# Two transformer blocks on one core: the modulation's products moved from VectorE to f32 matmuls in four column groups

## The reference

```python
c_act = jax.nn.silu(c)                       # [1, 2048]
mod = c_act @ w_ada[l] + b_ada[l]            # w_ada: [2048, 12288], 100.7 MB
sh1, sc1, gt1, sh2, sc2, gt2 = jnp.split(mod, N_MOD, axis=-1)
h = modulate(rmsnorm(x, g_norm_mix[l]), sh1, sc1)     # h * (1 + scale) + shift
proj = h @ w_in[l]
...                                          # conv, gated recurrence, pooling
x = x + gt1[:, None, :] * y                  # y = mixed @ w_out
h = modulate(rmsnorm(x, g_norm_ffn[l]), sh2, sc2)
f = (jax.nn.silu(h @ w_ffn_gate[l]) * (h @ w_ffn_up[l])) @ w_ffn_down[l]
x = x + gt2[:, None, :] * f
```

## Time and profile before

| | |
|---|---|
| median of three runs | 2662.82 us |
| span of the profiled execution | 2662.5 us |
| its time beyond the span | none is reported apart; the span is 0.3 us under the median |
| PE busy | 2521.5 us, 95% |
| DVE busy | 1904.7 us, 72% |
| ACT busy | 1183.1 us, 44% |
| moved by DMA | 553.91 MB, mean 208 GB/s |

### The profile page before, as it was taken

How to read it: one execution, slowest core, us unless ns; L and a number is a source line. 1 busy time by engine, 2 the same in 40 slices (tenths; PEclk the granted TensorE clock), 3 DMA queues, 4 the chain that set the end, 5 groups by cost and what they waited for, 6 DMA issues and landing times.

```text
span 2662.5 us, 38962 instructions
## 1 busy us (share of the span) xinstructions
PE 2521.5 (95%) x14020; PEld 2142.7 (80%) x14020; DVE 1904.7 (72%) x2383; ACT 1183.1 (44%) x1437; POOL 9.8 (0%) x37
## 2 busy tenths in 40 slices
PE   1399998999999999999999999999999999999997
PEld 0286676888888888888888888888888888888886
DVE  7899887865555555577677565576788758875886
ACT  1154434444444444464344455455544444444443
POOL 1000000000000000000000000000000000000000
PEclk9999998999999999999999999999999999999998
DMA  9888996965555555565555455565555555565553
GB/s 359 328 314 286 341 335 231 338 214 185 186 187 183 189 184 188 162 193 180 172 177 168 160 169 191 190 183 190 180 186 185 189 180 185 182 196 182 189 170 114
DMA packets 158485, 553.91 MB, mean 208 GB/s; under 512 B 18337, under 2 KB 22433, under 8 KB 158385
## 3 DMA queue, kind: packets, MB, share of 16 engines
q1 hardware_dynamic: 156384, 549.85, 60.8%
q0 software_dynamic: 848, 2.69, 0.3%
q10 hardware_dynamic: 1152, 0.03, 0.0%
HBM read 550.38 MB, written 2.10 MB: 208 GB/s over the span
## 4 chain that ended last, share of the span: by engine, by line
PE 89%; DVE 8%; issue 2%; ACT 1%; DMA 1%; DVEq 0%; SPq 0%; ACTq 0%
PE ps L499 54%; PE ps L501 27%; DVE acc L1104 4%; PE ps L494 2%; PE ps L496 1%; PE pm L534 1%; DVE split L1060 1%; PE pm L544 1%; DMA x_t<-in_x_fm 0%; ACT split L764 0%; DVE xc L1259 0%; DVE ssq L1141 0%; PE pm L649 0%; DVE val L1175 0%; PE pm L594 0%
## 5 line engine op out<-in xcount | busy, mean ns | idle before, releaser
L1060 DVE TENSOR_TENSOR split<-raw,split 128x1024 fp32r<-128x1024 f32 (+1 forms) x864 | 1032.3, 1203 | 660.4 <-ACT split L764 658.2
L764 ACT ACTIVATE split<-raw 128x1024 fp32r<-128x1024 f32 (+1 forms) x864 | 897.7, 1043 | 1205.0 <-PE ps L501 1106.0
L499 PE MATMUL ps<-h_s,split 128*128 128x512 f32 x3904 | 1383.6, 399 | 16.1 <-DVE h_s L1169 7.2
L501 PE MATMUL ps<-h_s,split 128*128 128x256 f32 x3904 | 1094.4, 280 | 0.0
L499 PEld LDWEIGHTS ps<-h_s,split 128*128 128x128 f32 x3904 | 734.8, 188 | 208.9 <-issue 20.0
L499 PE MATMUL ps<-mid_s,split 128*128 128x512 f32 x2368 | 836.9, 399 | 0.2 <-DVE split L1060 0.2
L501 PEld LDWEIGHTS ps<-h_s,split 128*128 128x128 f32 x3904 | 738.6, 189 | 0.5
L501 PE MATMUL ps<-mid_s,split 128*128 128x256 f32 x2368 | 663.5, 280 | 0.0
L499 PEld LDWEIGHTS ps<-mid_s,split 128*128 128x128 f32 x2368 | 444.8, 188 | 121.8 <-issue 12.1
L501 PEld LDWEIGHTS ps<-mid_s,split 128*128 128x128 f32 x2368 | 446.8, 189 | 0.0
L771 ACT ACTIVATE low<-ps 128x512 f32<-128x512 f32 x224 | 129.9, 580 | 4.4 <-PE ps L501 4.4
(11 more groups left out here) (222 smaller groups left out, 1155.2 us busy)
## 6 DMA issues: line engine op xcount, KB each, us to landing
raw<-in_w_in SPq DMA_DIRECT2D x224, 512.0 KB, 3.3
ride<-in_w_ada_late SPq DMA_DIRECT2D x128, 512.0 KB, 5.6
raw<-in_w_ffn_down SPq DMA_DIRECT2D x128, 512.0 KB, 3.3
raw<-in_w_ffn_gate SPq DMA_DIRECT2D x88, 512.0 KB, 3.3
raw<-in_w_ffn_up SPq DMA_DIRECT2D x88, 512.0 KB, 3.4
raw<-in_w_ffn_a SPq DMA_DIRECT2D x88, 512.0 KB, 4.1
raw<-in_w_ffn_b SPq DMA_DIRECT2D x88, 512.0 KB, 4.4
ada<-in_w_ada SPq DMA_DIRECT2D x64, 512.0 KB, 5.8
```

Of the source, the lines that this page charges most:

```text
L499: pe.matmul(ps[:, s, b, :], split[:, slot, k, 0, b * P:(b + 1) * P], acts[:, k0 + k, :, :].rearrange("p h t -> p (h t)"), start=start, sto ...
L501: mm = pe.matmul(ps[:, s, b, 0:T], split[:, slot, k, 1, b * P:(b + 1) * P], acts[:, k0 + k, 0, :], start=False, stop=stop)
L764: act.activation(split[:, c, 0:kt, 0, :], raw[:, CHUNKS * s + c, 0:kt, :], ACT.Copy).then_inc(hi_ready, 1)
L1060: dve.tensor_tensor(split[:, c, 0:kt, 1, :], raw[:, CHUNKS * s + c, 0:kt, :], split[:, c, 0:kt, 0, :].bitcast(F32), ALU.subtract).then_inc ...
```

## The change

- All 12 parts are multiplied on PE. A piece is now two row tiles, 1 MB, and there are 96 of them (8 for each part). For each of its two row tiles `e` and column halves `h`, one f32 product with a stationary operand of 32 columns (`c_pad`: column 0 is the activation's, 31 are zero) writes 32 partitions of one PSUM bank, from partition 32 * (2h + e). So the four products of a piece lie in four column groups of the array.
- At a part's end ACT copies the bank to `row` (128 by 512), and four f32 products with the two-column selector `sel` add the two row tiles and turn the row; DVE adds the bias. The row's DMA is gone.
- Before slab 0 come the parts in the order 2, 0, 3, 1, with a ring of 5 pieces. Parts 2 and 0 are scale and shift of features 0 to 1023, so the first 8 blocks are normed before the other two parts are in.
- The 64 later pieces ride at 8 in 12 chunks (parts 4 to 9 in `ADA_ORDER`'s order, from slab 0) and then 8 in 16 chunks (slabs 20 to 28), with a ring of 3.
- The last part alone keeps the old layout in memory; its pieces are read with a stride of 8 elements.
- The first norm's sum of squares and the pooling's products change PSUM banks.

```diff
-def _rides():
-    at = {S: ([0, 1, 2, 3], []) for S in range(5)}
-    at.update({5: ([0, 1, 2, 3], [3]), 6: ([0, 1, 2, 3], [1, 2, 3])})
...
+    for n in range(EARLY, ADA_PARTS):
+        if n < 10:
+            at += [12 * (n - EARLY) + d for d in (0, 1, 2, 4, 5, 6, 8, 9)]
+        else:
+            at += [CHUNKS * 20 + 20 * (n - 10) + 2 * d for d in range(PIECES)]
...
+        for piece in range(EARLY * PIECES):
+            if piece >= EARLY_RING:
+                sp.wait_ge(ada_multiplied, piece - EARLY_RING + 1)
+            load_ada(piece % EARLY_RING, piece // PIECES, piece % PIECES)
...
+            for r, at in enumerate(RIDE_AT):
+                if at == G - RAW:
+                    sp.wait_ge(ada_multiplied, EARLY * PIECES + max(r - LATE_RING + 1, 0))
+                    load_ada(r % LATE_RING, EARLY + r // PIECES, r % PIECES)
...
+        def multiply_ada(n, i, slot, times):
+            if i == 0 and n > 0:
+                pe.wait_ge(row_copied, n)
+            pe.wait_ge(ada_loaded[slot], 16 * times)
+            piece = ada_slot(slot)
+            for e in range(2):
+                for h in range(2):
+                    g = 32 * (2 * h + e)
...
+                    mm = pe.matmul(pm[2][g:g + 32, :], c_pad[:, 2 * i + e, :], moving,
+                                   start=(i == 0), stop=(i == PIECES - 1))
+            mm.then_inc(ada_multiplied, 1)
+        def turn_ada(n):
+            pe.wait_ge(row_copied, n + 1)
+            if n >= 1:
+                pe.wait_ge(mod_ready, n)
+            for j in range(4):
+                mm = pe.matmul(pm[3][:, 2 * j:2 * j + 2], row[:, j * P:(j + 1) * P], sel[:, :], start=True, stop=True)
+            mm.then_inc(ada_turned, 1)
...
+        def ride_along(G):
+            for r, at in enumerate(RIDE_AT):
+                if at == G:
...
+                    multiply_ada(EARLY + r // PIECES, r % PIECES, slot, before + r // LATE_RING + 1)
+            for n, at in LAST_RIDE.items():
+                if at + 2 == G:
+                    turn_ada(n)
...
+        def copy_row(n):
+            act.wait_ge(ada_multiplied, PIECES * (n + 1))
+            if n >= 1:
+                act.wait_ge(ada_turned, n)
+            act.activation(row[:, :], pm[2][:, :], ACT.Copy).then_inc(row_copied, 1)
...
-        for k in range(DB):
-            add_first(0, k)
...
+        finish_ada(0)
+        finish_ada(1)
+        dve.wait_ge(mod_ready, 2)
+        modulated_gain(1, "g_norm_mix", 0, LB)
+        norm(0, 0, range(LB))
+        finish_ada(2)
```

More of the change, by code:

```diff
@@ L64 @@
 ADA_PARTS = N_MOD * D // ADA_COLS
-ADA_FIRST = 4
-ADA_RING = 8
-RIDE_RING = 5
-def _rides():
-    at = {S: ([0, 1, 2, 3], []) for S in range(5)}
-    at.update({5: ([0, 1, 2, 3], [3]), 6: ([0, 1, 2, 3], [1, 2, 3])})
[L74 to L79, removed]
-RIDE_AT = _rides()
[L83 to L109, removed]
+ADA_FIRST = ADA_PARTS - 1
+RIDE_PARTS = range(ADA_FIRST, ADA_PARTS)
+ADA_ORDER = (2, 0, 3, 1, 4, 5, 8, 6, 9, 7, 10, 11)
+PIECES = DB // 2
+EARLY = 4
+EARLY_RING = 5
+LATE_RING = 3
+def _rides():
+    at = []
+    for n in range(EARLY, ADA_PARTS):
[3 more added lines that the diff above has]
+            at += [CHUNKS * 20 + 20 * (n - 10) + 2 * d for d in range(PIECES)]
+    return at
+RIDE_AT = _rides()
+LAST_RIDE = {n: RIDE_AT[PIECES * (n - EARLY) + PIECES - 1] for n in range(EARLY, ADA_PARTS)}
+RIDE_SLABS = (LAST_RIDE[ADA_PARTS - 1] + 3) // CHUNKS + 1
 IN_ORDER = [*range(0, 4), *range(8, 12), *range(4, 8)]
@@ L842, in _ @@
         act.activation(lam_e[:, :], lam_p[:, :], ACT.Exp, scale=-1.0).then_inc(lam_exp, 1)
-        convert(0, 0, 0)
-        norm(0, 0, 0, convert_first=True)
+        copy_row(0)
+        copy_row(1)
+        for b in range(LB):
+            norm_block(0, 0, b)
+        copy_row(2)
+        convert(0, 0, 0)
+        copy_row(3)
+        for b in range(LB, DB):
+            norm_block(0, 0, b)
+            if b in (8, 11, 14):
+                convert(0, 0, (b - 5) // 3)
         def sigmoids(q):
@@ L1135, in add_squares, with finish_rides @@
+        def finish_rides(S, c):
+            for n, at in LAST_RIDE.items():
+                if at + 3 == CHUNKS * S + c:
+                    finish_ada(n)
         def add_squares(n, j):
@@ L1160, in inv_rms, with norm @@
             inverse(n)
-        def norm(n, k, shift, convert_first=False):
-            if n > 0:
-                inv_rms(n)
+        def norm(k, shift, blocks, after=lambda b: None):
             def lo(b):
@@ L1171, in lo @@
                                          in1=h_s[:, b, 0, :].bitcast(F32), op0=ALU.add, op1=ALU.subtract).then_inc(h_ready, 1)
-            for b in range(DB):
+            for b in blocks:
                 if b >= 4:
@@ L1419, in mid @@
                     y_low(3)
[L1420 removed]
+                finish_rides(S_OUT + q, c)
             return mid
```

248 lines of the change are left out of this document (91 added, 157 removed).

## The result

| | kernel before | changed kernel |
|---|---|---|
| median, us | 2663.64 (10 runs, 2660.01 to 2664.94) | 2669.09 (10 runs, 2666.48 to 2672.81) |
| ratio to before, 95% interval | | 1.0023 [1.0014, 1.0032] |
| span of the profiled execution, us | 2662.5 | 2669.3 |

The changed kernel is slower by 5.5 us, 0.2%. The forecast was 2671. The profile's page after, in the order of the earlier trace rows: busy times, then PE, DVE, PE's granted clock and the transfer rate in 40 slices.

What follows compares the result with a forecast made beforehand. DVE was taken to bound the first 120 us and PE the rest. From 2662.5 us, less 18, 3.7 and 56, plus 76.8 for pieces and 9.6 for turns, came 2671 us, range 2649 to 2757.

Steps and rivals of the forecast that it cites:

- the formula: Whole kernel: 2662.5 less 18, 3.7 and 56 us, plus 64 riding pieces and 8 turns at their costs, giving 2671.2.
- start, to slab 0's end without its pieces: Before and in slab 0: without its three pieces, slab 0 ends at 120.8 us against 138.5, a gain of 18.
- 64 pieces: Riding pieces newly on PE beside the slabs: 1.2 us each, 76.8 us in all.
- 8 turns: Turns on PE beside the slabs: eight records each, taken at 1.2 us, 9.6 us in all.
- What bounds it: DVE bounds the first 120 us; then PE does, its waits for DVE and riding loads summing to 3.7 us.
- Slab 0 starts at 104.5: Before slab 0: with transfers at 410 GB/s as the bound, it starts at about 104.5 us instead of 120.28.
- The new wait of 2.7 us: In slab 0: PE asks for the first riding load at 109.6 us, but it lands at 112.3, so PE waits 2.7.
- X = 1.2: Cost of one riding piece on PE: four products abreast in four column groups take 1.2 us; chance 32%.
- rival B: Riding pieces: strict record order keeps groups in line, five steps, 2.43 us a piece, 2750 us in all; chance 28%.
- The stride at 0: Last part's 8 pieces: strided reads may cost 0 to 7 us, taken as 0 since no row shows them.
- The transfers under the rides: Riding loads beside the slabs cost nothing: 1 MB lands in at most 11.2 us, within 14.8 us of cover.

Runs made afterwards that it cites:

- the plain layout: Changed kernel with the last part laid out and read in a row like the others, without the stride of 8 elements: 2671.24 us, ratio 1.0025 to the kernel before.
- the versions with cheaper items on PE: Kernel before with PE's riding pieces and turns in two column groups: 2647.51 us; the same plus the changed kernel's start: 2633.85 us.
- the second execution: The changed kernel profiled once more, with nothing changed: 2666.96 us.
- the version of both together: Kernel before with the changed kernel's start and its own PE rides put in two column groups: 2633.85 us, ratio 0.9874 to the kernel before.

## Why the prediction was right

Right in its mechanism, and in its total partly by luck: what the sum missed by slab 30 (8.1 us too little) was taken back by a step of PE that it had no term for (10.5 us). At slab 30's end, where the last item of either modulation is done, the formula gives +8.7 us and the traces +16.8:

| term, us | forecast | measured | moves the sum by |
|---|---|---|---|
| start, to slab 0's end without its pieces | -18 | -13.6 | +4.4 |
| 64 pieces | 76.8 (1.2) | 72.3 (1.13) | -4.5 |
| 8 turns | 9.6 (1.2) | 7.7 (0.96) | -1.9 |
| stride of the last part | 0 | 8.0 | +8.0 |
| slabs 21 to 24 of before at the faster step | 0 | 4 x 0.21 | +0.8 |

Together +6.8, which makes 15.5; 1.3 us stay without a term. (Measured start: 138.48 - 128.27 + 3 x 1.13; the other executions with the same start give up to 14.7. Stride: slabs 25 to 28 in the trace of the changed kernel less the same in that with the plain layout.)

- **What bounds it.** Right. The two stretches were to be read apart, and the start gave back what PE's extra work took only in part. DVE's relief of 200 us could give little: PE's waits for it and for riding loads had been 3.7 us in all. How near DVE was to being the bound in slabs 0 to 9 (96% busy from 120 to 240 us) the prediction didn't say; the versions with cheaper items on PE show it.
- **Slab 0 starts at 104.5.** It was 103.6, with transfers at 409 GB/s for the 410 of the forecast.
- **The new wait of 2.7 us.** The load landed as worked out (112.7 for 112.3). PE asked earlier, at 108.2 and not 109.6, since the slow pace lasted 3 us and not a chunk. In the second execution it lasted the chunk, and the wait was 2.83 us, as forecast. But the step left out that the work behind the wait runs slowly: in the first execution the piece and the chunk behind it, by 0.9 and 1.7 us. That, 1.8 us of longer wait and 1.3 us from the last product to ACT's copy, which the sum forgot, less the 0.9 of the start and 0.6 of the first chunk, makes 4.2 of the 4.4.
- **X = 1.2.** It was 1.13. The reasoning from separate columns and outputs held for four f32 products abreast, and the second record of a product doesn't hold the next product back, as rival B had it: four records start at 280.0 us and four at 280.5. The speedup that the Trainium skill ("TensorE: Matmul & The Clock Gate", Part 3: Packing small matmuls) gives for four row tiles, 3.07, would have made X 1.40. Here four column groups gave 3.62 / 1.06 = 3.4 times the speed of one, two gave 1.9 times; no run has row tiles.
- **The stride at 0.** The term that failed: "no row shows strided reads, I take 0", with 0 to 7 as bounds. It cost 8.0, the doubling that the upper bound named. The Trainium skill ("SBUF — State Buffer", Door 1: The DMA port swizzle) states that reads in one 16-byte line run at full rate and that each step into a new line pays; eight f32 elements are 32 bytes, and the trace agrees, 2.14 us for 1.11. That page was not weighed beforehand.
- **What the formula has no term for.** The step of plain slabs: slabs 31 to 79 at 0.21 us less gave back 10.5 us. Only so did the span's difference come down from 16.8 us to 6.8, and the medians' to 5.5, near the forecast's 8.7. This part is luck, and the plain layout shows it: 8 us taken out, nothing gained.

The transfers under the rides were hidden as argued: after the first riding piece PE waited for no riding load, up to 575 us.

## What to carry to other kernels

Where PE is the bound, small f32 products beside its main stream cost what their column groups make them cost: put independent ones in different groups first (a few lines gave 0.7% here), and only then ask which engine should do the rest. Move work onto the engine that is the bound only where the trace shows it waiting for the other one, as PE waited for DVE in slabs 0 to 9; elsewhere every item is paid in full. Price a new wait of PE of some microseconds with the slow products behind it. And before a difference of under 0.5% is given to a change, compare the stretches of both traces that the change doesn't touch, and profile each kernel twice.

## What the runs showed of the hardware

- Four f32 products of a 32-column operand in four column groups take 1.06 us together, two groups 1.91, one 3.62, for the same eight records.
- A moving f32 operand read with a stride of 8 elements takes about twice the time: 2.14 us a piece against 1.13 in four groups, 4.08 against 2.0 in two, 7.66 against 3.7 in one.
- After PE's waits of 4.3 and 4.5 us its products ran at the pace of 1.2 GHz for about 5 us (granted clock 0.50 from 112.7 to 118 us in the changed kernel, 0.76 from 240 to 250 us in the version of both together). After the wait of 2.83 us in the second execution the piece took 1.07 us, and then the slab's products took 0.63 us each for 3.3 us.
- Plain slabs take either 11.09 or 11.31 us for dozens of slabs on end, at a granted clock of 1.00 and without a gap. Which one repeats from execution to execution of a program in most stretches (not in slabs 157 to 171), and changes between programs that do the same there. It is worth 10 us in this kernel, more than the change. The cause is open.
- The transfers held 409 GB/s for 68 us in pieces of 1 MB.
